# Two blocks in one kernel: delta-rule transfers, joins, folds and norm products put in another order

## The reference, cut to what matters

```
first_block:  h = rmsnorm(x);  proj = h @ w_in            (4112 columns)
  attention:  8 heads of 64, window of 8 x 16 in a grid of 16 x 64, relative bias, gated by silu(az)
  delta rule: q, k, v = silu(conv5(...)); q, k L2-normed; 4 heads of 128, forward and backward
     per chunk:  g = cumsum(g);  decay = exp(g_i - g_j) on the lower triangle
                 A = strict(kb k^T * decay) + I ;  u, w = A^-1 [v*beta, kb*exp(g)]
                 intra = (q k^T) * decay
     scan over chunks:  v_new = u - w S;  o = (q*exp(g)) S + intra v_new
                        S = S*exp(g_last) + (k*exp(g_last-g))^T v_new
     o = rmsnorm(o_f + o_b) * silu(dz)
  x = x + concat(attn, delta) @ w_out
second_block: x += 0.5*swiglu(rmsnorm(x))                  (d_ff 2752)
  u = rmsnorm(x) @ w_in2;  fourier mixer on 512 columns; grouped-query attention:
     8 query heads, 2 key heads, q and k rmsnormed and rotated, softmax over all 1024 keys
  x += concat(f, a) @ w_out2;  x += 0.5*swiglu(rmsnorm(x));  out = rmsnorm(x)
```

## Time and profile before

| | |
|---|---|
| median of 3 runs | 2815.33 us (2815.26 to 2818.02) |
| profiled execution | 2815.0 us, span 2813.2 us |
| TensorE busy | 2673.6 us (95%), 13337 matmuls |
| VectorE busy | 1178.2 us (42%) |
| ScalarE busy | 1066.2 us (38%) |
| GpSimd busy | 1237.8 us (44%) |
| granted TensorE clock, mean | 0.980 |
| DMA | 273.20 MB, mean 97 GB/s |
| chain that ended last | TensorE 82%, VectorE 7%, GpSimd 4%, ScalarE 3%, DMA 2% |

### The profile page before, as it was taken

The page is one execution under the profiler, slowest core; times in us unless marked ns, Lnnn a source line. Parts: engine busy times, 40 slices in busy tenths (PEclk is TensorE's granted clock), DMA queues, the critical chain, the costliest instruction groups (busy, mean ns, idle before and its releaser), DMA issues.

```text
span 2813.2 us, 33037 instructions
## 1 busy us (share of the span) xinstructions
PE 2673.6 (95%) x13337; PEld 2149.9 (76%) x13337; DVE 1178.2 (42%) x1634; ACT 1066.2 (38%) x1588; POOL 1237.8 (44%) x714
## 2 busy tenths in 40 slices
PE   8999998888879999999999998899999999999997
PEld 6788875577858888878888777666788888788885
DVE  7575657664663222222222328666532222222223
ACT  5434346534544322233322323655452222232222
POOL 2222213653036545556545555311564545564544
PEclk9999998999989999999999999999999999999998
DMA  4224215441153222332232332000323232323331
GB/s 148 91 83 156 91 53 189 157 143 31 38 170 107 98 98 91 104 105 98 98 97 91 104 125 86 38 9 1 109 90 101 95 100 91 111 98 101 121 100 68
DMA packets 93880, 273.20 MB, mean 97 GB/s; under 512 B 25944, under 2 KB 26136, under 8 KB 93600
## 3 DMA queue, kind: packets, MB, share of 16 engines
q1 hardware_dynamic: 93728, 271.09, 28.6%
HBM read 240.05 MB, written 31.00 MB: 96 GB/s over the span
## 4 chain that ended last, share of the span: by engine, by line
PE 82%; DVE 7%; POOL 4%; ACT 3%; DMA 2%; issue 1%; SPq 1%; POOLq 0%; DVEq 0%; ACTq 0%
PE ps L350 23%; PE ps L352 23%; PE ps L351 23%; PE ps L880 2%; PE ps L900 2%; PE ps L864 2%; ACT t L366 2%; POOL t L1341 1%; POOL t L1338 1%; PE ps L498 1%; DVE t L1014 1%; PE ps L1442 1%; POOL t L1839 1%; POOL t L415 1%; ACT t L963 1%
## 5 line engine op out<-in xcount | busy, mean ns | idle before, releaser
L366 ACT ACTIVATE t<-t 128x1024 fp32r<-128x1024 f32 (+5 forms) x961 | 736.1, 810 | 1392.9 <-PE ps L352 648.5
L415 POOL TENSOR_TENSOR t<-t 128x1024 fp32r<-128x1024 f32 x356 | 864.0, 2431 | 874.5 <-ACT t L366 874.5
L350 PE MATMUL ps<-t 128*128 128x512 f32 (+1 forms) x3034 | 1198.5, 395 | 32.7 <-POOL t L415 17.5
L351 PE MATMUL ps<-t 128*128 128x512 f32 (+1 forms) x3034 | 1181.4, 389 | 0.0
L352 PE MATMUL ps<-t 128*128 128x512 f32 (+1 forms) x3034 | 1181.1, 389 | 0.0
L350 PEld LDWEIGHTS ps<-t 128*128 128x128 f32 x3034 | 572.2, 189 | 166.3 <-issue 47.3
L351 PEld LDWEIGHTS ps<-t 128*128 128x128 f32 x3034 | 572.4, 189 | 121.4 <-issue 6.5
L352 PEld LDWEIGHTS ps<-t 128*128 128x128 f32 x3034 | 572.1, 189 | 119.0
L2055 DVE SCALAR_TENSOR_TENSOR t<-ps,t 128x512 f32<-128x512 f32 x192 | 132.7, 691 | 317.8 <-PE ps L352 277.1
L2111 POOL TENSOR_TENSOR t<-t 128x512 fp32r<-128x512 f32 x84 | 108.8, 1296 | 332.3 <-ACT t L366 332.3
L2032 DVE TENSOR_TENSOR t<-ps,t 128x512 f32<-128x512 f32 x84 | 58.1, 692 | 396.6 <-PE ps L352 396.6
(11 more groups left out here) (167 smaller groups left out, 1873.7 us busy)
## 6 DMA issues: line engine op xcount, KB each, us to landing
t<-in_wts_dram SPq DMA_DIRECT2D x356, 512.0 KB, 3.5
t<-pj SPq DMA_DIRECT2D x39, 512.0 KB, 5.7
pj<-t SPq DMA_DIRECT2D x32, 512.0 KB, 2.7
t<-in_rpb_dram SPq DMA_DIRECT2D x8, 736.0 KB, 7.8
t<-in_xT_dram SPq DMA_DIRECT2D x8, 512.0 KB, 8.2
t<-grow_d SPq DMA_DIRECT2D x8, 512.0 KB, 8.6
t<-beta_d SPq DMA_DIRECT2D x8, 512.0 KB, 9.7
t<-in_xT_dram SPq DMA_DIRECT2D x16, 256.0 KB, 3.8
```

Source lines behind the costliest of these rows:

```text
L350: e.matmul(out, ah, bh, start=start, stop=False)
L351: e.matmul(out, ah, bl, start=False, stop=False)
L366: return e.activation(out, in_, fn, scale=scale)
L415: e.tensor_tensor(lo[:], T.raw[n % NR][:], hi[:].bitcast(F), SUB).then_inc(*w_lo.up(n))
```

## The change

1. The blocks R and Y of a head (batch 0: of both heads) become one tensor each, so a gather transfer takes both directions of a head (8 transfers instead of 16) and a scatter transfer takes all four chains of batch 0 or both of a head of batch 1 (4 and 8 instead of 16 and 16).
2. The first inverse starts at place 19 and gives 2, 3, 3, 3 steps at places 0, 1, 2, 3 modulo 4. The gate products of NA go from places 14, 22, 30, 38 to 14, 22, 35, 38; head 2's scaled rows from 37 to 34, its exponentials from after NA to 34, its differences from 33 to 32.
3. SyncE: the store and scatter of batch 0 and the rows of head 3 go ahead of park(2) and the load of query 3; kt(0) goes behind the second gather and block load.
4. The backward chains' F result is multiplied by beta in one VectorE operation instead of eight ScalarE copies.
5. Joins go from places 6 to 15, two each, to places 8 to 15 with 2, 2, 3, 3, 3, 3, 2, 2 units.
6. In attention `aside(i)` goes ahead of the j=0 transposes (NA's is empty).
7. In the last down group of a feed-forward block the first two outputs do all but the last tile first.
8. Second in-projection: query 0's norm steps 2 to 4 on ScalarE move from tile 6 to tile 7, its sum's copy on VectorE from behind to ahead of the fold.

```diff
...
     D_.dm = sb(early, [128, 4, 128], side="right")
-    D_.R, D_.Y, D_.D = ([[sb(early, [128, L], side="right") for _ in range(2)] for _ in range(2)] for _ in range(3))
+    D_.D = [[sb(early, [128, L], side="right") for _ in range(2)] for _ in range(2)]
+    D_.RR, D_.YY = [sb(early, [128, 4, L], side="right")], [sb(early, [128, 4, L], side="right")]
...
         two_heads = lambda: [[sb(st, [128, L]) for _ in range(2)] for _ in range(2)]
-        one_head = lambda: [[sb(st, [128, L]) for _ in range(2)]]
         D_.k += [sb(st, [128, L]) for _ in range(2)]
-        D_.R, D_.Y = D_.R + one_head(), D_.Y + one_head()
+        D_.RR.append(sb(st, [128, 2, L]))
+        D_.YY.append(sb(st, [128, 2, L]))
...
         D_.D += two_heads()
-        D_.R = D_.R + one_head()
+        D_.RR.append(sb(st, [128, 2, L]))
         sb(st, [128, 896])
-        D_.Y = D_.Y + one_head()
+        D_.YY.append(sb(st, [128, 2, L]))
         D_.X = two_heads() + two_heads()
         D_.blocks = [sb(st, [128, L]) for _ in range(3)]
+        D_.R, D_.Y = ([[T[0][:, 2 * h + i, :] for i in range(2)] for h in range(2)] + [[t[:, i, :] for i in range(2)]
+                                                                                   for t in T[1:]] for T in (D_.RR, D_.YY))
...
                 spread(g)
+            aside(i)
             if 0 <= i - 1 < n:
                 transposes(pairs[i - 1], 0)
-            aside(i)
...
+    NA_GATES = [14, 22, 35, 38]
...
             pool_delta_early(e, w, i)
-            if i == 37:
+            if i == 34:
                 for d in range(2):
                     scaled_row(e, w, 2, d)
-            if i >= 14 and (i - 14) % 8 == 0:
-                c = (i - 14) // 8
+            if i in NA_GATES:
+                c = NA_GATES.index(i)
...
         e.dma_start(q_first[2], pj[18]).then_inc(*q_load[0].up(2))
-        park(2)
-        e.dma_start(q_first[3], pj[19]).then_inc(*q_load[1].up(3))
...
         sp_rows(e, w, 3)
+        park(2)
+        e.dma_start(q_first[3], pj[19]).then_inc(*q_load[1].up(3))
...
     (d_diff, d_mt, d_in, l_p1, l_x1, l_y1, s_r, s_S, s_O, o_add, o_var, o_f0, o_f1, o_n,
-     o_out) = kinds("delta_dve", 15)
+     o_out, d_tb_v) = kinds("delta_dve", 16)
...
     early_row = lambda i: divmod((i - 6) // 2, 2) if 6 <= i < 14 and (i - 6) % 2 == 0 else None
-    first_inverse, inverse_rate = 20, 3
+    first_inverse, inverse_rate = 19, [2, 3, 3, 3]
...
     JOINS, todo_ = {}, [("T", a) for a in range(4)] + LEVELS
-    for i_ in range(6, 16):
-        JOINS[i_], todo_ = todo_[:2], todo_[2:]
+    for i_, n_ in enumerate((2, 2, 3, 3, 3, 3, 2, 2)):
+        JOINS[i_ + 8], todo_ = todo_[:n_], todo_[n_:]
...
+    def decays(e, w, h):
+        for d in range(2):
+            w.wait_ge(d_diff, (h, d))
+            act(e, D_.D[h][d][:], D_.D[h][d][:], ACT.Exp).then_inc(*d_exp.up((h, d)))
     def act_delta_early(e, w, i):
+        if i == 34:
+            decays(e, w, 2)
...
     def dve_delta_early(e, w, i):
-        if i == 33:
+        if i == 32:
...
         if first_inverse <= i < first_inverse + 16:
-            for _ in range(inverse_rate):
+            for _ in range(inverse_rate[i % 4]):
...
-    def block_of(b, a, i):
-        return lambda dram: dram[b].rearrange("(g t b) (j i) -> g b j t i", t=8, b=4, i=32)[a, i]
+    def blocks_of(dram, b, first, count, i):
+        return dram[b].rearrange("(g t b) (j i) -> g b j t i", t=8, b=4, i=32)[first:first + count, i].rearrange(
+            "g j t i -> j g t i")
+    def diagonal(T, i):
+        k = slice(32 * i, 32 * i + 32)
+        return T.rearrange("p g (t f) -> p g t f", t=8)[k, :, :, k]
     def sp_gather(e, w, b):
-        for a in range(4):
-            h, d = chain(b, a)
-            w.wait_ge(*((d_mt, (h, d)) if d == 0 else (d_r1, h)))
+        for x in range(2):
+            h = 2 * b + x
+            w.wait_ge(d_mt, (h, 0))
+            w.wait_ge(d_r1, h)
+            T = D_.RR[0][:, 2 * h:2 * h + 2, :] if b == 0 else D_.RR[h - 1][:]
             for i in range(4):
-                k = slice(32 * i, 32 * i + 32)
-                e.dma_start(block_of(b, a, i)(rb_d), v8(D_.R[h][d])[k, :, k]).then_inc(*gath.up((b, a, i)))
+                e.dma_start(blocks_of(rb_d, b, 2 * x, 2, i), diagonal(T, i)).then_inc(*gath.up((b, x, i)))
...
         w.wait_ge(wb_store, b)
-        for a in range(4):
-            h, d = chain(b, a)
-            w.wait_ge(d_zero, (h, d))
+        for h in (2 * b, 2 * b + 1):
+            w.wait_ge(d_zero, (h, 1))
+        for x, T in enumerate([D_.YY[0][:]] if b == 0 else [D_.YY[1][:], D_.YY[2][:]]):
+            n = 4 if b == 0 else 2
             for i in range(4):
-                k = slice(32 * i, 32 * i + 32)
-                e.dma_start(v8(D_.Y[h][d])[k, :, k], block_of(b, a, i)(wb_d)).then_inc(*scat.up((b, a, i)))
+                e.dma_start(diagonal(T, i), blocks_of(wb_d, b, n * x, n, i)).then_inc(*scat.up((b, x, i)))
...
                     p = place(r, ("2",) + key, [(s_vn, key)])
-                    w.wait_ge(d_tb, (h, d))
+                    w.wait_ge(d_tb_v if d else d_tb, (h, d))
...
                 e.tensor_tensor(Y_[:], Y_[:], r[("y",) + key], SUB).then_inc(*l_y1.up(key))
+            if what == "F" and d == 1:
+                w.wait_ge(l_x1, key)
+                e.tensor_tensor(v8(X_), v8(X_), bcl(beta[:, :, hd_of(h, d)]), MUL).then_inc(*d_tb_v.up((h, d)))
...
     def act_delta(e, w):
-        def decays(h):
-            for d in range(2):
-                w.wait_ge(d_diff, (h, d))
-                act(e, D_.D[h][d][:], D_.D[h][d][:], ACT.Exp).then_inc(*d_exp.up((h, d)))
...
                 m.then_inc(*d_kd.up((h, d)))
-            if what == "F":
-                w.wait_ge(*((l_y1, (h, d, 1)) if d == 0 else (l_x1, (h, d, 1))))
+            if what == "F" and d == 0:
+                w.wait_ge(l_y1, (h, d, 1))
...
-        decays(2)
         for a in range(4):
             first_x(0, a, slots_d)
         backward(2)
-        decays(3)
+        decays(e, w, 3)
...
         q_again(0)
-        kt(0)
         sp_gather(e, w, 1)
         sp_blocks_in(e, w, 1)
+        kt(0)
...
+    def down_order(s, g, nk):
+        all_ = tuple(range(nk))
+        if (s, g) == (1, final_group):
+            return [(0, all_[:-1]), (1, all_[:-1]), (0, all_[-1:]), (1, all_[-1:])] + [(o, all_) for o in range(2, KC)]
+        return [(o, all_) for o in range(KC)]
...
                 first, nk = P.first_of[i], GROUPS[i]
-                for o in range(KC):
+                for o, ks in down_order(s, i, nk):
                     nw = n + o // 2
                     hi, lo = weights_of(nw)
-                    p = pe_slot(w, (P.name, s, i, o), [P.x_ready(s, i, o)], banks)
-                    w.wait_ge(w_lo, nw)
-                    for k in range(nk):
+                    if ks[0] == 0:
+                        pe_slot(w, (P.name, s, i, o), [P.x_ready(s, i, o)], banks)
+                        w.wait_ge(w_lo, nw)
+                    p = banks[P.name, s, i, o]
+                    for k in ks:
...
                             m = e.matmul(p, lo[0:64, a], ah[0:64, :], start=False, stop=True)
-                    m.then_inc(*(w_used.up(nw) if o % 2 else b_dn.up((P.name, s, i, o))))
+                    if ks[-1] == nk - 1:
+                        m.then_inc(*(w_used.up(nw) if o % 2 else b_dn.up((P.name, s, i, o))))
...
                     act_norm(e, w, K, 10)
-                if (s, m) == (1, 6):
+                if (s, m) == (1, 7):
...
                     dve_factor(e, w, "mixn", 1)
+                if (s, m) == (1, 6):
+                    dve_norm(e, w, Q0, 1)
...
                         dve_norm(e, w, K, step)
-                if (s, m) == (1, 6):
-                    dve_norm(e, w, Q0, 1)
```

## The result

The changed kernel takes 2790.75 us (median of 3 runs, 2786.17 to 2791.96) against 2815.33: a ratio of 0.9905, with a 95% interval of 0.989 to 0.9921. The forecast was 2784.5. The profiled execution took 2791.96 us with a span of 2790.2, so its ledger has 23.0 us instead of the forecast 30.5. A later series of the same kernel gave 2789.47 (4 runs, 0.9901), with a profile of 2787.77 us and a span of 2786.0.

A forecast was written before the change was run, and what follows sets the result against it. TensorE, busy 95% of the span, was taken as the bound, so only its idle time and lower clock could be won. Gains of 15.2 + 7.0 + 3.3 + 1.0 + 4.0 = 30.5 from 2815.0 gave 2784.5 us, range 2772 to 2800.

The forecast's parts named there:

- NA's diagonals: Neighbourhood attention: the earlier inverse takes 1.9 us off TensorE's 4.3 us wait for GpSimd's diagonals, bounds 0 and 4.3.
- First scatter: Delta stage's start: four larger transfers and an earlier store remove the 7.87 us wait; about 3 us for VectorE remains.
- Second scatter: Delta stage: eight transfers of double size bring the data in 5.9 us against 9.14, leaving a 2.0 us wait.
- Backward fold: First scan's start: VectorE products replace 16 ScalarE copies, fourth operand about 2.9 us earlier, bounds 1.5 and 4.7.
- Joins from place 8: First scan: one more 5.35 us step before the scatter's wait, dense end net 0; delta stage gains 15.2 in all.
- Attention: Grouped-query attention: norm products ahead of transposes gain 1.0 per sum and 1.5 per rotation; 7.0 us taken, bounds 2 and 8.6.
- Second in-projection: Last tile: the 5.51 us wait for weights goes; gain 4.0 less 0.7 for the clock, 3.3 us, bounds 1 and 6.4.
- Last group: Feed-forward down products: reordering fills the half tile's wait, gaining 1.0 us in the first block and 4.0 at the end.
- the dense end is not paid back: Rival, chance 0.1: each three-unit join place waits for ScalarE or VectorE, 7 us in all, giving 2792.
- The clock stays up: Rival, chance 0.14: waits of about 2 us do not lower the clock in delta stage and in-projection; +9, 2776.
- The fourth head's chain is late: Rival, chance 0.2: queue traffic keeps the second gather where it was; delta stage gains 9.5 instead of 15.2, giving 2790.
- the 24 us of the rival: Rival, chance 0.04: big gather and scatter transfers use few DMA engines; with two, 4096 packets take 24 us, giving 2848.

The follow-up runs named there:

- a_inv: Changed kernel with the first inverse beginning at place 20 again, three steps a place: 2791.16 us, ratio 0.9911 to the kernel before.
- a_split: Changed kernel with gathers and scatters in the small transfers of before, on the new layout: 2794.44 us, ratio 0.9917.
- after: The changed kernel with all edits, in its first series, against the kernel before: 2790.75 us, profiled execution 2791.96 us.
- after_again: The changed kernel unaltered, measured and profiled again in a later series: 2789.47 us, ratio 0.9901.
- a_fold: Changed kernel with the backward fold of beta on ScalarE as before, instead of two VectorE products: 2788.9 us, ratio 0.9897.
- a_join6: Changed kernel with joins from the first scan's place 6 again, two units a place: 2789.65 us, ratio 0.9902.
- i_early_end: Changed kernel with the 20 joins as 2, 2, 4, 3, 3, 2, 2, 2, denser places earlier: 2785.61 us, ratio 0.9888.
- a_aside: Changed kernel with attention's norm sums and rotations behind the four transposes again: 2794.11 us, ratio 0.9916.
- a_down: Changed kernel with the last group's down product in plain order in both feed-forward blocks: 2794.29 us, ratio 0.9923.

## Why the prediction came close, and where it missed

The direction, the places and most terms held, and the time came out inside the range (2772 to 2800). In part that was luck: the second in-projection gave 2.3 us more than forecast where the delta stage, attention and the end gave 6.8 less. Point by point, forecast against the ledger:

- **NA's diagonals** 1.9: 2.2, shown by a_inv; the wait fell from 4.3 to 2.2 us.
- **First scatter.** The step held: the wait moved to VectorE's mask product (3.19; about 3 forecast). The reason given for the 7 us was half wrong: the size of the transfers hardly matters there, the store's place does (a_split). The low clock charged behind it came in six executions of twelve. Of the order of the rows, parks and kt no experiment undid anything; the store's part is read from the traces alone.
- **Second scatter** 5.9 us from issue to data: 5.83, and 9.16 when split.
- **Backward fold** 2.9 earlier at the scan's start, in full gain: this step failed. It put the start of the scan forward in front of a longer wait: 5.36 us for the scatter, not 2.0. The times of after are 2.0 us late from ahead of NA2, so they are counted here from the keys' product (576.90; 575.2 in the forecast). TensorE reached place 8 at 80.7 us instead of 84.3: the low clock charged at the stage's start did not come in this execution, and the waits at the scan's start fell from 5.6 to 2.0 us, more than 2.9. The data came at 86.0, and 86.3 was forecast, but by luck. Head 3's product was 1.8 us early through the clock. The gather (1.0 us for 0.4 charged), the inverse (42.6 against 41.0, 1.6 for 1 charged) and the store's landing (3.3 us, 2.75 before) took that back. In after_again, with the low clock at the start, the data came at 88.4. a_fold puts the edit at -1.0 us.
- **Joins from place 8**, +5.35 with the tail's 2.4 us "given back": this is the step that cost most. The wait came as forecast (2.50), but nothing gave it back, and a low clock came with it; a_join6 puts the edit at 0 (after with the low spell in its tail, a_join6 without one), and i_early_end shows 3.3 us lying in the three-unit place near the end. Delta with NA: 12.5 us for 15.2 forecast.
- **Attention** 7.0: 4.9, and 5.3 by a_aside. The rotations gained 1.5 each as forecast, the sums 0.8 instead of 1.0 and the first 0.6. What the forecast left out is that the first sum's products, moved ahead, fall into the low clock behind the stage's first wait: 3.77 us instead of 1.98. Where the clock had risen in time the stage gained 6.7 to 7.0.
- **Second in-projection** 3.3: 5.6. The forecast kept the last norm step at the 3.28 us it took beside GpSimd; it took 1.28 (2.0), and the 0.7 charged for the clock did not come.
- **Last group** 1.0 and 4.0: 1.1 and 2.0 in the profile of after, 2.0 and 3.0 by a_down. The end gained from 2.0 to 4.0 us in the twelve profiles with the edit. In after the half tile came 0.9 us later behind the attention's end than before, ahead of anything that the edit moves, and the second output is complete 1.8 us after the half tile (5.5 before), where the forecast has 1.1. The sums of squares then follow TensorE at 2.22 us each, because a longer spell at the lower clock had put TensorE behind; in six of the twelve profiles they keep the 2.09 us forecast.

The sum by the ledger is 12.5 + 1.1 + 5.6 + 4.9 + 2.0 = 26.0 (26.1 with the rounded terms); less the 2.0 that this execution lost ahead of NA2 it is 24.0, as the starts of the final product have it (2799.18 - 2775.18). That product took 2.05 us instead of 1.10, which leaves 23.0 of the span. Of the rivals, "the dense end is not paid back" (2792, given 0.1) is what happened in mechanism, at one place and not at each. "The clock stays up" came half true: at the stage's start in six executions of twelve, and at the in-projection's end in all but a_down, but not behind the scatter. "The fourth head's chain is late" has 2790, the time that was measured, and is still refuted: the second gather's load was issued 34.4 us after the keys' product and not 40.4, so the gather did not stay where it was.

## What to carry to other kernels

When a wait is followed by a longer one for something else, shortening the first gains nothing until the second is short, as a_fold shows; ask what the thing behind the second wait hangs on (here one mask product of VectorE, moved by one unit: 4.4 to 5.5 us) and pay for that first. When work is packed more densely behind a wait, keep the engines that hand over to the next phase light in the last places: the same 20 units cost 3.3 us more with a three-unit place there, low clock included. To judge a part of 1 to 5 us, time stages between fixed instructions in several profiles instead of whole runs.

## What the runs showed of the hardware

The low clock did not follow the length of a wait alone. Behind the same wait of 3.17 to 3.19 us the clock stayed up in six executions (8.96 us to head 2's keys' product) and fell in six others (10.5 to 11.8). The delta stage of kernels that differ only elsewhere still took 219.6 to 220.3 us, for the spell came behind the tail's wait instead. Nine profiles have the tail's wait of 2.50 us: the clock fell behind it in the three where it had stayed up at the start (3.47 to 3.62 us for sixteen matmuls), and stayed up in the six where it had fallen there (2.02). Why that is so stays open. A single profile therefore can't price a low spell at one place.

The issue of a transfer of 128-byte pieces takes 0.48 us for 256 pieces, 0.51 for 512 and 0.56 to 0.63 for 1024, and it lands 1.8, 2.2 and 3.4 us after its issue. Queue and landing added up, an estimate, four transfers do in about 5.6 us (2.22 + 3.4) what sixteen do in 9.5 (7.72 + 1.8). The 32 partitions stayed the slowest dimension, and by the Trainium skill, "DMA: Bandwidth & Descriptors", section "Why a DMA increments its semaphore by 16 and not by 1", the engines stay 16 then. The landing times agree: 3.4 us where two engines would need the 24 us of the rival.
